# A hybrid decoder step on one Trainium2 core: four MLP projections in one block, and another order of state slots

## What is computed

```python
def sq_relu_mlp(h, w_up, w_down):
    return jnp.square(jax.nn.relu(h @ w_up)) @ w_down

    yp = yp + att_p @ w_out[i]
    ys = ys + att_s @ w_out[i]
    yp = yp + sq_relu_mlp(rms_norm(yp, g_mlp[i]), w_up[i], w_down[i])
    ys = ys + sq_relu_mlp(rms_norm(ys, g_mlp[i]), w_up[i], w_down[i])
```

## Time and profile before

| | us |
|---|---|
| median of 3 runs | 3617.67 (3616.65 to 3619.46) |
| the profiled execution | 3616.07 |
| its span, first to last instruction | 3613.9 |
| TensorE busy with matmuls | 3230.2 (89%) |
| VectorE busy | 1593.3 (44%) |
| ScalarE busy | 1273.7 (35%) |
| GpSimd busy | 201.4 (6%) |
| mean granted TensorE clock | 0.934 of full |

### The profile page before, as it was taken

How to read it: one execution, slowest core, us unless ns; L and a number is a source line. 1 busy time by engine, 2 the same in 40 slices (tenths; PEclk the granted TensorE clock), 3 DMA queues, 4 the chain that set the end, 5 groups by cost and what they waited for, 6 DMA issues and landing times. The chain is left out here.

```text
span 3613.9 us, 56580 instructions
## 1 busy us (share of the span) xinstructions
PE 3230.2 (89%) x23847; PEld 3013.6 (83%) x23847; DVE 1593.3 (44%) x1683; ACT 1273.7 (35%) x1302; POOL 201.4 (6%) x140
## 2 busy tenths in 40 slices
PE   7799999774677999999999999966789999999999
PEld 5699999553346999999999999954389999999999
DVE  4543334354554544333443354344555443344433
ACT  3432224243564433333332242235134333333322
POOL 0000000022330000000000000023200000000000
PEclk9899999887788999999999999967789999999999
DMA  4545353404654445454545545301654545545453
GB/s 150 181 156 185 118 161 112 143 1 159 195 181 136 156 155 163 151 163 156 168 148 168 165 149 167 128 32 49 218 176 144 162 150 163 165 161 164 150 165 132
DMA packets 317268, 537.10 MB, mean 149 GB/s; under 512 B 18245, under 2 KB 115519, under 8 KB 316104
## 3 DMA queue, kind: packets, MB, share of 16 engines
q1 hardware_dynamic: 316440, 529.73, 45.2%
q10 hardware_dynamic: 624, 4.46, 0.3%
HBM read 517.23 MB, written 25.19 MB: 150 GB/s over the span
## 5 line engine op out<-in xcount | busy, mean ns | idle before, releaser
L469 DVE TENSOR_TENSOR project_weights_low<-ring,project_weights_high 128x2048 fp32r<-128x2048 f32 x344 | 788.5, 2292 | 1203.8 <-ACT project_weights_high L404 1203.8
L404 ACT ACTIVATE project_weights_high<-ring 128x2048 fp32r<-128x2048 f32 x344 | 658.6, 1915 | 1265.0 <-PE project_banks L334 1264.9
L332 PE MATMUL project_banks<-high,project_weights_high 128*128 128x288 f32 x2560 | 763.6, 298 | 37.4 <-DVE project_weights_low L459 33.5
L333 PE MATMUL project_banks<-low,project_weights_high 128*128 128x288 f32 x2560 | 761.6, 297 | 0.0
L334 PE MATMUL project_banks<-high,project_weights_low 128*128 128x288 f32 x2560 | 761.3, 297 | 0.0
L332 PE MATMUL project_banks<-up_high,project_weights_high 128*128 128x288 f32 x2048 | 609.9, 298 | 27.5 <-DVE project_weights_low L459 27.5
L333 PE MATMUL project_banks<-up_low,project_weights_high 128*128 128x288 f32 x2048 | 608.7, 297 | 0.0
L334 PE MATMUL project_banks<-up_high,project_weights_low 128*128 128x288 f32 x2048 | 608.6, 297 | 0.0
L332 PEld LDWEIGHTS project_banks<-high,project_weights_high 128*128 128x128 f32 x2560 | 488.2, 191 | 39.5 <-DVE project_weights_low L459 34.8
L333 PEld LDWEIGHTS project_banks<-low,project_weights_high 128*128 128x128 f32 x2560 | 488.1, 191 | 0.0
L334 PEld LDWEIGHTS project_banks<-high,project_weights_low 128*128 128x128 f32 x2560 | 486.7, 190 | 0.0
(11 more groups left out here) (517 smaller groups left out, 3059.8 us busy)
## 6 DMA issues: line engine op xcount, KB each, us to landing
ring<-in_w_up_dram SPq DMA_DIRECT2D x128, 1024.0 KB, 5.2
ring<-in_w_down_dram SPq DMA_DIRECT2D x128, 1024.0 KB, 5.1
ring<-in_gla_w_in_dram SPq DMA_DIRECT2D x40, 1024.0 KB, 5.1
h<-in_cache_nsa_kv_dram SPq DMA_DIRECT2D x256, 128.0 KB, 2.3
ring<-in_w_out_dram SPq DMA_DIRECT2D x32, 1024.0 KB, 5.2
ring<-in_nsa_w_in_dram SPq DMA_DIRECT2D x28, 1024.0 KB, 5.1
sp_keys_values<-in_cache_nsa_kv_dram SPq DMA_DIRECT2D x80, 256.0 KB, 3.8
ring<-in_w_mem_kv_dram SPq DMA_DIRECT2D x16, 1024.0 KB, 5.2
```

The lines of the kernel that those rows point to most:

```text
L332: nc.tensor.matmul(bank, w_high, moving_high[:, kt], start=(kt == 0), stop=False)
L333: nc.tensor.matmul(bank, w_high, moving_low[:, kt], start=False, stop=False)
L404: nc.scalar.activation(weights_high[:, c % 2], g.ring[:, c % RING], ACT.Copy).then_inc(rounded, 1)
L469: nc.vector.tensor_tensor(weights_low[:, c % 2], g.ring[:, c % RING], weights_high[:, c % 2].bitcast(F32), ALU.subtract).then_inc(split, 1)
```

## The change

`project` becomes a call of `projects` with one job. `projects` opens one block, one pair of PSUM halves and one pair of weight-part buffers for a list of jobs, and each engine runs the jobs' programs one behind the other. `feed_forward` hands it the four MLP projections of a layer. Cut to its core:

```diff
+def projects(nc, g, base, jobs):
+    with ExitStack() as ctx:
...
+        for n, (job, options) in enumerate(jobs):
+            programs.append(project_programs(nc, g, ctx, base, banks, positive, weights, programs[-1] if n else None,
+                                             n == len(jobs) - 1, *job, **options))
+            base = programs[-1].end
+        block = ctx.enter_context(nc.Block())
+        @block.tensor
+        def _(pe):
+            for p in programs:
+                p.tensor(pe)
...
     def tensor(pe):
         def group(n, half):
             wait(pe, banks_free, n - 1)
+            if earlier is not None and isinstance(n, int) and n < 2:
+                pe.wait_ge(earlier.banks_free, earlier.groups - 1 + n)
             for c in range(chunks):
+                if earlier is not None and earlier.lows is not None and is_first(n):
+                    pe.wait_ge(earlier.lows, c + 1)
                 if not is_first(n, c):
                     pe.wait_ge(split, n * chunks + c)
...
     def scalar(act):
...
                 if is_first(n, c):
                     act.wait_ge(g.weights_loaded[0], 16 * (base // RING + 1))
+                    if earlier is not None:
+                        act.wait_ge(g.weights_used, base - 1)
...
+                if c == 1 and is_first(n) and earlier is not None:
+                    earlier.scalar_leave()
...
-            leave(groups - 1)
+        if is_last:
+            leave(groups - 1)
...
     def vector(dve):
...
+                if c == 1 and is_first(n) and earlier is not None:
+                    earlier.vector_leave()
+                if c == 2 and is_first(n) and earlier is not None:
+                    earlier.vector_leave_low()
```

`lows` counts the subtractions that make `up_low` (L439). In `feed_forward`:

```diff
+        jobs = []
         for n in range(2):
-            base = project(nc, g, base, half // 4, KT, up_chunks[n], ("square relu", up), parts=parts,
...
-            base = project(nc, g, base, 4, half, down_chunks[n], ("add", g.x), parts=up,
...
+            jobs.append(((half // 4, KT, up_chunks[n], ("square relu", up)),
...
+            jobs.append(((4, half, down_chunks[n], ("add", g.x)),
...
+        base = projects(nc, g, base, jobs)
```

In `linear_outputs`, the slots and the sync engine's part:

```diff
-        slots = [in_ring[:, n] for n in range(3)] + [in_p[:, n] for n in range(3)]
+        slots = [in_p[:, 0], in_p[:, 1], in_ring[:, 0], in_ring[:, 1], in_ring[:, 2], in_p[:, 2]]
+        IN_RING = (2, 3, 4)
...
             for m in range(PAIRS):
+                if m == PAIRS - 1:
+                    for b in IN_RING:
+                        sp.wait_ge(stored[b], 16)
+                    load_first_chunks(sp, g, next_chunks, base)
                 sp.wait_ge(state_taken, of_pair(m + 1))
...
             for b in range(BATCH):
                 sp.wait_ge(stored[b], 16)
-            load_first_chunks(sp, g, next_chunks, base)
```

More of the change, by code:

```diff
@@ L235, in load_other_chunks, with project, _, project_programs @@
         group(groups - 1, late_source)
-def project(nc, g, base, groups, k_tiles, src, then, moving=None, parts=None, next_chunks=None, late=(0, None),
-            gain=None, normed=False, few=None, also=None):
+def project(nc, g, base, *job, **options):
+    return projects(nc, g, base, [(job, options)])
+def projects(nc, g, base, jobs):
+    with ExitStack() as ctx:
+        banks = ctx.enter_context(nc.psum_tensor(f"project{base}_banks", [P, 2, 4, 512], F32))
+        positive = ctx.enter_context(nc.sbuf_tensor(f"project{base}_positive", [P, 4, TOKENS], F32)) \
+            if jobs[0][0][3][0] == "square relu" else None
+        weights = [None, None]
+        programs = []
+        for n, (job, options) in enumerate(jobs):
[3 more added lines that the diff above has]
+        block = ctx.enter_context(nc.Block())
+        @block.sync
+        def _(sp):
+            for p in programs:
+                p.sync(sp)
+        @block.tensor
+        def _(pe):
+            for p in programs:
+                p.tensor(pe)
+        @block.scalar
+        def _(act):
+            for p in programs:
+                p.scalar(act)
+        @block.vector
+        def _(dve):
+            for p in programs:
+                p.vector(dve)
+    return base
+def project_programs(nc, g, ctx, base, banks, positive, weights, earlier, is_last, groups, k_tiles, src, then,
+                     moving=None, parts=None, next_chunks=None, late=(0, None), gain=None, normed=False, few=None,
+                     also=None):
     chunks = k_tiles // WTILES
@@ new lines, in project_programs @@
+    assert earlier is None or not normed
+    if parts is None:
+        parts = [ctx.enter_context(nc.sbuf_tensor(f"project{base}_{name}", [P, k_tiles, TOKENS], F32R))
+                 for name in ("high", "low")]
+    moving_high, moving_low = parts
+    if weights[0] is None:
+        weights[:] = [ctx.enter_context(nc.sbuf_tensor(f"project{base}_weights_{name}", [P, 2, WTILES, WCOLS], F32R))
+                      for name in ("high", "low")]
+    weights_high, weights_low = weights
+    if few is not None:
+        few_src, few_col, few_n, few_out = few
+        w_few = ctx.enter_context(nc.sbuf_tensor(f"project{base}_few", [P, KT, few_n], F32))
+        few_high, few_low = (ctx.enter_context(nc.sbuf_tensor(
+            f"project{base}_few_{name}", [P, KT, few_n], F32R)) for name in ("high", "low"))
@@ new lines, in project_programs @@
+    banks_free, positive_squared, square_rounded, rounded, moving_rounded, split, first_rounded, first_split, \
+        squared, added, summed, mean, root, inverse, few_loaded, few_rounded, few_split, few_done, lows = map(
+            counters(nc, ctx, f"project{base}_"), (
+                "banks_free", "positive_squared", "square_rounded", "rounded", "moving_rounded", "split",
+                "first_rounded", "first_split", "squared", "added", "summed", "mean", "root", "inverse",
+                "few_loaded", "few_rounded", "few_split", "few_done", "lows"))
@@ new lines, in project_programs, with over_groups @@
+    rms = g.rstd[:].rearrange("p (a n) -> p a n", a=2)
+    sums = banks[:, 1, 0:2, 0:TOKENS // 2]
+    own_squares = banks[:, 1, :, 0:TOKENS]
+    squares = positive if kind == "square relu" else g.h[:, 0:WTILES]
+    rstd = g.rstd[:].unsqueeze(1).to_broadcast([P, 4, TOKENS])
+    few_bank = banks[0:few[2], groups % 2, 0, 0:TOKENS] if few is not None else None
+    def over_groups(eng, group):
+        group(0, 0)
+        group(1, 1)
+        with eng.Fori(1, groups // 2) as m:
+            group(m * 2, 0)
+            group(m * 2 + 1, 1)
+        if groups % 2:
+            group(groups - 1, 0)
@@ new lines, in tiles_of, with is_first, gain_of, sync @@
+    def tiles_of(c):
+        return slice(c * WTILES, (c + 1) * WTILES)
+    def is_first(n, c=0):
+        return isinstance(n, int) and n == 0 and c == 0
+    def gain_of(kt):
+        return g.vec[:, gain + kt:gain + kt + 1]
+    def sync(sp):
+        if few is not None:
+            sp.dma_start(w_few[:], few_src.rearrange("(k p) n -> p k n", p=P)[:, :, few_col:few_col + few_n]
+                         ).then_inc(few_loaded, 16)
+        load_other_chunks(sp, g, src, base, groups, chunks, late)
+        if also is not None:
+            also(sp)
+        if next_chunks is not None:
+            load_first_chunks(sp, g, next_chunks, base + groups * chunks)
@@ new lines, in tensor, with group @@
+    def tensor(pe):
+        def group(n, half):
+            wait(pe, banks_free, n - 1)
+            if earlier is not None and isinstance(n, int) and n < 2:
+                pe.wait_ge(earlier.banks_free, earlier.groups - 1 + n)
+            for c in range(chunks):
+                if earlier is not None and earlier.lows is not None and is_first(n):
+                    pe.wait_ge(earlier.lows, c + 1)
+                if not is_first(n, c):
+                    pe.wait_ge(split, n * chunks + c)
+                for k in range(WTILES):
+                    if is_first(n, c):
+                        pe.wait_ge(first_split, k + 1)
+                    kt = c * WTILES + k
+                    for o in range(4):
+                        w_high = weights_high[:, c % 2, k, o * P:(o + 1) * P]
+                        w_low = weights_low[:, c % 2, k, o * P:(o + 1) * P]
+                        bank = banks[:, half, o, 0:TOKENS]
+                        nc.tensor.matmul(bank, w_high, moving_high[:, kt], start=(kt == 0), stop=False)
+                        nc.tensor.matmul(bank, w_high, moving_low[:, kt], start=False, stop=False)
+                        mm = nc.tensor.matmul(bank, w_low, moving_high[:, kt], start=False,
+                                              stop=(kt == k_tiles - 1))
+                mm.then_inc(g.weights_used, 1)
+            if is_first(n) and normed:
+                pe.wait_ge(added, chunks - 1)
+                for half_of in range(2):
+                    for k in range(WTILES):
+                        mm = nc.tensor.matmul(sums[:, half_of], g.ones[:], squares[
```

(81 more changed lines are left out.)

270 lines of the change are left out of this document (67 added, 203 removed).

## The result

The changed kernel took 3570.78 us (median), the kernel before 3617.67, which is the median without one slow run of 3903.97 us. That is 46.9 us less; the ratio is put at 0.9867, with a 95% interval of 0.9847 to 0.9886. The profiled execution took 3570.71 us with a span of 3568.9, against 3616.07 and 3613.9. The prediction of 3571 us was right, and so was the way to it in the main.

A forecast was written before the change was run, and what follows sets the result against it. TensorE, busy 89% of the span, was taken to bound the kernel. Closing six seams gives -46.94 us (33.46 idle, 13.48 slow chunks), the states 0: 3571 us from 3617.67, range 3567 to 3584.

The forecast's parts named there:

- the seams: Six places, ahead of four `down` and two second `up` projections, where TensorE idles between blocks; 85.16 us long together.
- The sum: Joined block -46.94 us, new waits and states 0; from the median of 3617.67 this gives 3570.8, said as 3571.
- the reading that the slowness belongs to a projection's start: Rival at the first chunks: the clock stays slow at a job's start, only 33.46 us go, 3584; chance 0.03.
- The clock: First chunks after the seams: slowness comes from idle time, so its 13.48 us go too and the whole 46.94 is taken.
- The order at a seam: New weights' quarters are rounded during the last chunk, the old group's leftover work follows chunk 1's split; no stall.
- its room: At chunk 2 of the new projection: its split ends 0.62 us before TensorE wants it.
- The new waits: On TensorE's queue, one for banks in each of two groups and eight for `lows`: taken at 0.
- The bound for such a wait: TensorE's only wait for a queue after a barrier, 1.7 us; 0 to 10 us over six seams.
- The states: States' block, renamed slots and earlier `w_out` loads: 0, bounds 0 and 3 us; late-stores rival 3574, chance 0.01.
- The term beneath: End of the states' block: 8.9 MB pass in 25 us, done by 2639 with a completion; VectorE ends 5.5 us later.
- the slower rival: Joined stretch: without pauses TensorE's clock is granted less; 46.9 us given back at 0.98, 3694 at 0.95; chance 0.02.
- no seam was left over: Rival ahead of `down`: waits for `lows` or banks keep four seams, only 9.91 us go, 3608; chance 0.02.

The follow-up runs named there:

- the run with the old order: Changed kernel, one block, but each projection takes its last group out completely before the next one's first rounding; 3610.9 us against 3617.49 before.
- the run with the states alone: Kernel before, with only the states' slots and the early loads of w_out changed, every projection in its own block; 3617.3 us against 3617.49.
- the run with late rounding: Changed kernel, but a joined projection's first four quarters are rounded only when the last chunk before is counted; 3580.09 us, 9.3 more.
- the run with added matmuls: Changed kernel plus unused matmuls, five or nine, where TensorE stands idle at three block ends; 3575.61 us against 3571.18 on the same chip.

## Why the prediction was right

*What bounds.* Right: the seams were six of the twelve places where TensorE waited for L459, and these six are gone. In the changed kernel TensorE waits for L459's successor once in each MLP, at its start. The costliest helper by busy time was not ScalarE's rounding (658.6 us) but VectorE's split L469 (788.5 us); since that waited for the rounding, and the rounding for TensorE, the conclusion stands.

*The sum.* Predicted 46.94 us by counts; the two MLPs lost 46.69. The small rest is in the main that a seam was read from VectorE's start to ScalarE's, which do not wake equally fast: on one count of the run with the old order VectorE starts at 1664.55 and ScalarE at 1664.61, and six times 0.06 is 0.36 us. The idle part and the slow chunks went together, 33.46 and 13.48 us by that reading, so the reading that the slowness belongs to a projection's start is out. The Trainium skill ("TensorE: Matmul & The Clock Gate", Part 1: The HAM clock gate) has it that idleness lowers the clock. The trace agrees with it: 1.00 in all six first chunks.

*The clock.* Taking the whole 46.94 us was right, but the reason that was drawn from the rows for it does not hold; as far as it rested on that, it was luck. The reason was that the first chunk took less after less idle time, 8.26 us after 3.06 against 9.44 after 6.84. In the earlier trace rows the first chunks of the third and the sixth seam, with 6.8 us of idle time ahead, took less still: 8.21 and 8.17 us. In the trace of the run with the states alone the first chunk after 3.06 us of idle time took 9.13 us, and the one after 6.83 us took 7.81. So how much a slow chunk loses does not follow the length of the idle time ahead of it, and what sets it stays open.

*The order at a seam.* Right in its steps and nearly in its room: 0.62 us expected for chunk 2, 0.7 seen. The new waits cost nothing that shows: the `down` matmuls have no idle time before them, and the six first chunks take 6.37 us each. The bound for such a wait was read too low, since TensorE's wait for a queue after a barrier was 1.7 us at L647 but 3.8 us at L1514; nothing came of it. Every seam lies behind the loop over the earlier projection's groups. The Trainium skill ("Runtime: NRT & Kernel Launch", Instruction fetch mechanics) says that a taken branch out of the prefetched window stalls the engine. No such stall shows at the six seams.

*The states.* Right at 0, shown by the run with that part alone. The term beneath was sized too large: SP was expected to end 5.5 us ahead of VectorE and ends 7.5 us ahead. The rate was right: the 8.9 MB landed 25.2 us after the first of them was issued (2589.93 to 2615.12), about 354 GB/s where 360 were taken. What did not show are the 2 us that were added for a completion, which no row gave.

*The rivals.* The joined stretch is at 1.00 for 822 us, so the slower rival fell; no seam was left over.

## What to carry to other kernels

Where one projection follows another, count a gap at its full price: the idle time, and the matmuls behind it that run at the low clock. Close it by giving the helpers the next stage's first work ahead of the last one's clean-up; one block with the old order gave 6.6 of 47 us here. Before paying for a higher clock, look whether the next chunk's operands would be ready: where a helper set the pace here, the slow clock cost about 0.3 us.

## What the runs showed of the hardware that was not expected

The clock can fall after the work has begun again. At the seam ahead of layer 0's second `up`, TensorE by stretches in the kernel before:

```profile
1667.13:1667.94 0.81, 0.81 (x6) 1.00 1.06 412
1667.94:1671.40 3.46, 3.46 (x16) 0.51 0.14 53
1671.40:1675.39 3.99, 3.99 (x31) 1.00 0.02 4
```

After 3.06 us of idle time the first six matmuls ran at 1.00, the next 3.46 us at 0.51 (that is 1.2 GHz), and then it was 1.00 again. The price of idle time is thus paid behind it, at this seam wholly so. At the same seam of the run with the states alone the clock was already at 0.86 in the idle time, and the chunk behind it at 0.67. In the runs above, 1.55 us of idle time left the clock at 1.00 through the whole next chunk (all six seams of the run with late rounding), while 2.10 us were followed by a chunk at 0.79, as were 3.06 us, and as was the stretch of 2.08 us with two matmuls in it in the run with added matmuls.
